# Order of loads and copies, and four banks of the first down product, in a two-layer decoder step

## The chip, the cores and the metric

The kernel is one program on one core of a Trainium2 chip. The metric is the time of one execution on the device, in microseconds. PE is TensorE, DVE is VectorE, ACT is ScalarE, POOL is GpSimd, and SP is SyncE, which here only issues the transfers.

## What is computed

One inference step of a decoder with two layers, for a prompt of 1024 tokens and 8 samples of 8 new tokens each that share the weights (width 1024, MLP width 4096). All data is float32.

```python
for layer in range(2):
    if layer == 0:   # one input projection; an mLSTM (4 heads) beside three dilated windowed attentions (8 heads each)
        mix_p = ab_output(h_a, oa, outs, lses, w_out_ab[j])          # prompt
        mix_s = ab_output(h_a, oa, outs, lses, w_out_ab[j])          # samples, with their caches
    else:            # windowed attention, 16 query heads on 2 key heads, with sinks
        mix_p = o.reshape(xp.shape[0], s_len, OUT_C) @ w_out_c[j]
        mix_s = o.reshape(xs.shape[0], t_len, OUT_C) @ w_out_c[j]
    xp = layer_norm(ALPHA * xp + mix_p, ln1_g[layer], ln1_b[layer])
    xp = layer_norm(ALPHA * xp + sq_relu_mlp(xp, w_up[layer], w_down[layer]), ln2_g[layer], ln2_b[layer])
    ...              # the same for xs
# sq_relu_mlp(x, w_up, w_down) = square(relu(x @ w_up)) @ w_down
```

The states and the keys and values to keep are outputs too.

## The kernel before, in words

The work is cut into stages, one after the other, each a block of five instruction streams (one for each engine) that meet at its end: the mLSTM; the three dilated attentions (tiles named `g_`); the samples' attention with the first output projection and norm (`sp_`); the first MLP (`f_`); the windowed attention (`c_`); its samples with the second output projection and norm (`wp_`); the second MLP (`f_` again). Tokens lie in nine tiles: eight prompt tiles of 128 rows and one sample tile of 64 rows, number NT = 8. Within a stage the order on each engine is the order of the code; semaphores hold an engine until another has come far enough. Eight PSUM banks are dealt out in fixed pools; PE can fill a bank only when DVE or ACT has emptied its last content.

Exact products come from splitting each factor: ACT rounds it (`hi`), DVE subtracts to get the rest (`lo`), and PE makes three passes. So every operand passes ACT and then DVE before PE can use it.

**Windowed attention** (lines 557 to 787). For tile n, PE computes scores, projects tile n + 1, transposes the input of tile n + 2, transposes the 32 probability blocks of tile n in 8 groups of 4 through the four banks of pool a (4 groups for tile 0), then the queries and keys of n + 1, then the weighted sum. ACT copies the even groups out, DVE the odd ones (lines 782 to 785). DVE's `x_rest(n + 2)` (line 780), the `lo` half of the input of tile n + 2, stands ahead of these copies. It isn't there for n = 7 and 8, which have no tile n + 2.

**First samples and projection** (lines 1954 to 2161). SP's loop over n issues, in this order: the stores of the sample result n - 1 to DRAM (`store_sample`, 8 small transfers), the loads for the merge, the store of the normed tile n - 2, the load of the residual input of tile n, then keys, mix and values. For n = 8 (`BD`) the samples' mix tile, which holds what was just stored, is loaded at line 2041, after all that, and behind the wait for the residual sum of tile 7 at line 2027. PE needs it for `mix_transposes(8)`, right after `project(7)`.

**Second samples and projection** (lines 1548 to 1848). SP loads the samples' projection, then mix tile 0, weight block 0, the samples' keys and values (1 MB), weight block 1, mix tile 1, weight block 2 (each block 1 MB, mix tiles 0.5 MB); block 3 follows when the first block is split (line 1568). ACT's order is fixed: mix tile 0, weight blocks 0 and 1, the copies of the transposed keys `kT` (lines 1716 to 1718), blocks 2 and 3. PE's scores need `kT`, and their first bank is one that these copies free.

**MLP** (lines 2373 to 2721). The hidden width goes in 16 groups of 256. PE makes `hidden(n)`, six units of 24 matmuls (two row blocks f by token ranges 0 to 383, 384 to 767, 768 to 1087), and `down(n)`, 18 banks (nine tiles by two halves of 512 columns), 6 matmuls in each, 4 for the sample tile; DVE adds each bank to the accumulator. The order is `hidden(0)`, `hidden(1)`, `down(0)`, `hidden(2)`, `down(1)` and so on, all after `hidden(0)` in a loop (line 2524). `hidden(1)` needs the up weights of group 1, which ACT can round only when `hidden(0)` has let go of the buffer. The tiles of `down` come in `ORDER` (line 2365): sample tile first, then 0 to 7. The last down product has its weights in the up buffers, so it waits until the last hidden product is through and they are split (`last_lo`); down product 14 covers four banks of that wait (lines 2530 to 2532). Then DVE adds and norms tile after tile in `ORDER`, with one fold more for the sample tile, and the stage ends with it.

Of the kernel before, what the change touches and what calls it, by code (L numbers as in the profile page):

```python
# [17 lines left out]
NT = SEQ // P  # L18
BD, TD = 8, 8
# [4 lines left out]
HB, DH = 8, 64  # L24
# [193 lines left out]
def attention(nc, env, name, groups, cfg):  # L218
# [13 lines left out]
    N = TILES * len(groups)  # L232
# [23 lines left out]
    def prob_banks(n):  # L256
        return H * spans(n) // 4
# [34 lines left out]
    with ExitStack() as ctx:  # L292
# [76 lines left out]
        with nc.Block() as block:  # L369
# [271 lines left out]
            def _(dve):  # L641
# [116 lines left out]
                for n in range(-1, N):  # L758
                    if attends(n):
                        maxima(n, 0)  # L760
                    if attends(n - 1):
                        o_out(n - 1)
                    if n >= 0 and n % TILES == NT and n + 1 < N:
                        rest_of_weights((n + 1) // TILES, 2)
                    if n + 1 < N:
                        z_out(n + 1, 0)
                        if n < 0:
                            if swa:
                                x_rest(1)
                            rest_of_weights(0, 2)  # L770
                        if attends(n) and HALVES == 2:
                            maxima(n, 1)
                        if (n + 1) % TILES == NT and n + 2 < N:
                            rest_of_weights((n + 2) // TILES, 0)
                        for c in range(1, NCH):
                            z_out(n + 1, c)
                            if c == (2 if swa else 1):
                                rope(n + 1)
                    if n + 2 < N and not (swa and n < 0):
                        x_rest(n + 2)  # L780
                    if attends(n):
                        for b in range(1, prob_banks(n), 2):
                            dve.wait_ge(*banks.full(n, "p", b))
                            dve.tensor_copy(pT[:, 4 * b:4 * b + 4, :].rearrange("p k t -> p (k t)"), bank(n, "p", b)[:, :])\
                                .then_inc(banks.free(n, "p", b)[0], 1)
                    if (n + 1) % TILES == NT and n + 2 < N:
                        rest_of_weights((n + 2) // TILES, 1)
# [668 lines left out]
def window_sample_and_projection(nc, env, cfg):  # L1456
# [7 lines left out]
    NTT = NT + 1  # L1464
# [24 lines left out]
    with ExitStack() as ctx:  # L1489
# [57 lines left out]
        with nc.Block() as block:  # L1547
            @block.sync
            def _(sp):
# [3 lines left out]
                def load_mix(n):  # L1553
                    sp.dma_start(mixt[n % 2][0:rows_of(n), :], cfg["mix"][n * P:n * P + rows_of(n), :]).then_inc(m_loaded[n % 2], 16)
# [2 lines left out]
                    sp.dma_start(staged(u), w_unit(cfg["wo"].rearrange("(k p) n -> p k n", p=P), u)).then_inc(w_loaded[u], 16)  # L1557

                sp.dma_start(new[:, :], cfg["zs"]).then_inc(new_loaded, 16)
                load_mix(0)  # L1560
                load_w(0)
                sp.dma_start(kv[:, :, :], cfg["cache"].rearrange("b s x h d -> s b (x h d)")).then_inc(kv_loaded, 16)
                load_w(1)
                load_mix(1)
                load_w(2)
                for h in range(HC):
                    sp.dma_start(sinkc[h * TD:(h + 1) * TD, :], cfg["sinks"][:, h:h + 1].to_broadcast([TD, 1])).then_inc(sink_loaded, 16)
                sp.wait_ge(w_lo, 1)
# [286 lines left out]
def sample_and_projection(nc, env, cfg):  # L1855
# [9 lines left out]
    NTT = NT + 1  # L1865
# [28 lines left out]
    with ExitStack() as ctx:  # L1894
# [58 lines left out]
        with nc.Block() as block:  # L1953
            @block.sync
            def _(sp):
# [62 lines left out]
                for n in range(NTT + 2):  # L2018
                    if 1 <= n <= BD:
                        store_sample(n - 1)  # L2020
                    if n + 1 < NT:
                        sp.wait_ge(products, n + 1)
                        load_groups(n + 1)
                    if n >= 2:
                        store(n - 2)
                    if 1 <= n < NTT:
                        sp.wait_ge(*banks.free(n - 1, "y", 1))
                        load_x(n)
                    if n + 2 < BD:
                        sp.wait_ge(*banks.full(n + 1, "k", NB - 1))  # L2030
                        load_keys(n + 2)
                    if n + 1 < NT:
                        sp.wait_ge(*banks.full(n, "m", 1))
                        load_mix(n + 1)
                    if n + 1 < BD:
                        sp.wait_ge(*banks.full(n, "o"))
                        load_values(n + 1)
                    if n == BD:
                        for par in range(2):
                            sp.wait_ge(ob_stored[par], 16 * HB * (BD // 2))  # L2040
                        load_mix(NT)
                        sp.wait_ge(*banks.full(BD - 1, "o"))
                        cfg["prefetch"](sp)
                        for m in range(4):
                            sp.wait_ge(stored[m % 2], 16 * (m // 2 + 1))
                            cfg["load_ahead"](sp, m)
# [315 lines left out]

NTOK = SEQ + NS
NPAD = (NT + 1) * P
ORDER = (NT,) + tuple(range(NT))
TOK_CHUNKS = [(0, 384), (384, 384), (768, 320)]
FG = 256
NFG = FF // FG
# [4 lines left out]
def mlp(nc, env, name, cfg):  # L2373
# [9 lines left out]
    with ExitStack() as ctx:  # L2383
# [45 lines left out]
        with nc.Block() as block:  # L2429
# [34 lines left out]
            def _(pe):  # L2464
# [40 lines left out]

                dn_flat = [w[:, :, :].rearrange("p f n -> p (f n)") for w in dn]

                def down(n, par):
                    pe.wait_ge(dn_lo.sem, dn_lo.done(n))
                    pe.wait_ge(h_lo.sem, h_lo.done(n, UP - 1))  # L2510
                    for b in range(DN):
                        pe.wait_ge(d_free.sem, d_free.done(n, b, back=4))
                        down_part(n, par, b, dn_flat, True, True).then_inc(d_full.sem, 1)

# [3 lines left out]
                for b in range(UP):  # L2518
# [2 lines left out]
                    hidden_unit(0, b)  # L2521
                    for n in ((4,), (5,), (6,), (7, 8), (), ())[b]:
                        x_transposes(n)
                with pe.Fori(0, NFG // 2 - 1) as i:
                    for par in range(2):
                        hidden(2 * i + par + 1)
                        down(2 * i + par, par)
# [14 lines left out]
            def _(act):  # L2542
# [46 lines left out]
                for b in range(UP + 1):  # L2589
                    if b < UP:  # L2590
                        relu(0, 0, b)
                    if b >= 1:
                        round_hidden(0, 0, b - 1)
                    for n in ((4,), (5,), (6,), (7, 8), (), (), ())[b]:
                        x_out(n)
                next_up(0)
                split_weights(0, dn_raw, dn[0], dn_loaded, None, dn_hi)
                with act.Fori(0, NFG // 2 - 1) as i:
                    for par in range(2):
                        step_(2 * i + par + 1, par ^ 1)  # L2600
# [24 lines left out]
            def _(dve):  # L2625
# [39 lines left out]
                            dve.tensor_tensor(a, a, d, ALU.add).then_inc(d_free.sem, 1)  # L2665

                def step_(n, par, first=False, more=True):
                    for b in range(UP):
                        hidden_rest(n + 1, par ^ 1, b)
                    dve.wait_ge(d_free.sem, d_free.done(n, 0, back=1))  # L2670
                    for i in range(NTT):
                        add(n, par, i, first)
                        if i == 2 and more:
                            rest(n + 2, up_raw, up, up_hi, up_lo)
                    rest(n + 1, dn_raw, dn, dn_hi, dn_lo)
# [16 lines left out]
                for b in range(UP):  # L2692
                    hidden_rest(0, 0, b)
                    for n in ((5,), (6,), (7, 8), (), (), ())[b]:
                        x_rest(n)
                rest(1, up_raw, up, up_hi, up_lo)
                rest(0, dn_raw, dn, dn_hi, dn_lo)
                dve.wait_ge(cleared, 1)
                step_(0, 0, first=True)
                with dve.Fori(0, NFG // 2 - 2) as i:  # L2700
# [239 lines left out]
```

## Time and profile before

| | |
|---|---|
| runs, median (lowest to highest) | 3292.88 us (3292.0 to 3296.89) |
| the profiled execution | 3288.4 us, its span 3286.6 us |
| PE matmul busy | 3071.8 us (93% of the span) |
| DVE busy | 1561.1 us (47%) |
| ACT busy | 902.1 us (27%) |
| mean granted TensorE clock | 0.959 |
| instructions | 46489 |

PE works nearly all the time, so what counts is the rest: stretches in which PE stands idle, and stretches at half clock. A matmul's busy time is longer than the distance to the next one, since they overlap; distances come from counts in a stretch. In a timeline row the bracket is the idle time before the instruction and what ended it.

### The profile page before, as it was taken

The numbers are of one execution on the slowest core, as the hardware profiler recorded it, in microseconds if no ns is written. First come the engines' busy times: TensorE is split into PE (matmuls) and PEld (weight loads), VectorE is DVE, ScalarE is ACT, GpSimd is POOL, SyncE is SP. The second block draws the span as 40 slices with busy tenths as digits, with TensorE's granted clock in tenths as the row PEclk, the third lists the DMA queues.
The fourth block names the chain that finished last, engine by engine and source line by source line (L and its number), as shares of the span: only waits on it lengthen the run. The fifth ranks groups of instructions, "written<-read, shape, count | busy, mean of one in ns | idle before, by whom it ended". The sixth has DMA issues, their size and how long they took to land. (4 is left out here: it accounts for less than half of the span.)

```text
span 3286.6 us, 46489 instructions
## 1 busy us (share of the span) xinstructions
PE 3071.8 (93%) x18199; PEld 2619.0 (80%) x18199; DVE 1561.1 (47%) x3277; ACT 902.1 (27%) x1905; POOL 195.0 (6%) x241
## 2 busy tenths in 40 slices
PE   8999699999996996999999999699797999999997
PEld 4666588788885875998999898588686899889986
DVE  1333543544435774344444446645554443444447
ACT  1222233333233433111121113444433111112113
POOL 0000000000000110100110010000000011001100
PEclk9999699999998997999999999899898999999999
DMA  6000231353788863110111011310421011101111
GB/s 212 20 19 16 52 130 45 113 202 132 262 262 282 284 220 109 52 51 29 48 51 51 26 64 43 119 38 28 152 87 39 26 51 51 51 26 51 51 38 68
DMA packets 134418, 300.09 MB, mean 91 GB/s; under 512 B 15048, under 2 KB 64392, under 8 KB 133192
## 3 DMA queue, kind: packets, MB, share of 16 engines
q1 hardware_dynamic: 134280, 298.19, 26.9%
q8 instruction: 93, 1.52, 0.2%
q14 instruction: 45, 0.37, 0.0%
HBM read 260.65 MB, written 93.34 MB: 108 GB/s over the span
## 5 line engine op out<-in xcount | busy, mean ns | idle before, releaser
L2482 PE MATMUL f_ps_u<-f_xT_hi,f_up_hi 128*128 128x384 f32 (+1 forms) x1536 | 507.9, 331 | 28.4 <-DVE f_up_lo L2637 12.1
L2482 PE MATMUL f_ps_u<-f_xT_hi,f_up_lo 128*128 128x384 f32 (+1 forms) x1536 | 506.3, 330 | 0.0
L2482 PE MATMUL f_ps_u<-f_xT_lo,f_up_hi 128*128 128x384 f32 (+1 forms) x1536 | 506.1, 329 | 0.0
L2652 DVE TENSOR_TENSOR f_hT_lo<-f_h,f_hT_hi 128x384 fp32r<-128x384 f32 (+1 forms) x192 | 146.1, 761 | 562.2 <-ACT f_hT_hi L2566 558.7
L2502 PE MATMUL f_ps_d<-f_dn_hi,f_hT_hi 128*128 128x512 f32 x1080 | 411.9, 390 | 1.3 <-DVE acc L2665 0.6
L2502 PE MATMUL f_ps_d<-f_dn_lo,f_hT_hi 128*128 128x512 f32 (+1 forms) x1080 | 411.7, 390 | 0.0
L2502 PE MATMUL f_ps_d<-f_dn_hi,f_hT_lo 128*128 128x512 f32 x960 | 373.9, 389 | 0.0
L2482 PEld LDWEIGHTS f_ps_u<-f_xT_hi,f_up_hi 128*128 128x128 f32 x1536 | 293.3, 191 | 31.2 <-issue 20.4
L2482 PEld LDWEIGHTS f_ps_u<-f_xT_lo,f_up_hi 128*128 128x128 f32 x1536 | 293.1, 191 | 1.1
L2482 PEld LDWEIGHTS f_ps_u<-f_xT_hi,f_up_lo 128*128 128x128 f32 x1536 | 292.8, 191 | 0.0
L2561 ACT ACTIVATE f_h<-f_ps_u 128x384 f32<-128x384 f32 (+1 forms) x192 | 91.0, 474 | 605.7 <-PE f_ps_u L2482 605.7
L524 PE MATMUL g_ps_b<-g_w_hi,g_xT_hi 128*128 128x512 f32 x648 | 255.3, 395 | 2.0 <-DVE g_xT_lo L655 2.0
L983 PE MATMUL m_ps_z<-w_m,m_xT 128*128 128x412 f32 (+3 forms) x800 | 248.7, 493 | 8.6 <-ACT m_xT L1106 5.9
L524 PE MATMUL g_ps_b<-g_w_lo,g_xT_hi 128*128 128x512 f32 (+1 forms) x648 | 251.8, 391 | 0.0
L2502 PEld LDWEIGHTS f_ps_d<-f_dn_hi,f_hT_hi 128*128 128x128 f32 x1080 | 202.8, 188 | 48.9 <-DVE acc L2665 1.9
L2502 PEld LDWEIGHTS f_ps_d<-f_dn_lo,f_hT_hi 128*128 128x128 f32 (+1 forms) x1080 | 196.3, 182 | 45.1
L2622 POOL TENSOR_TENSOR f_h<-f_h 128x384 f32<-128x384 f32 (+1 forms) x192 | 152.5, 794 | 1332.6 <-ACT f_h L2561 1332.6
L983 PEld LDWEIGHTS m_ps_z<-w_m,m_xT 128*128 128x128 f32 (+1 forms) x800 | 136.6, 187 | 114.3 <-issue 108.8
L524 PE MATMUL g_ps_b<-g_w_hi,g_xT_lo 128*128 128x512 f32 x576 | 225.4, 391 | 0.0
L2665 DVE TENSOR_TENSOR acc<-acc,f_ps_d 128x512 f32<-128x512 f32 x252 | 168.8, 686 | 104.1 <-PE f_ps_d L2502 104.1
L2502 PEld LDWEIGHTS f_ps_d<-f_dn_hi,f_hT_lo 128*128 128x128 f32 x960 | 180.2, 188 | 37.6
L2665 DVE TENSOR_TENSOR w_group<-w_group,f_ps_d 128x512 f32<-128x512 f32 x224 | 151.9, 686 | 102.6 <-PE f_ps_d L2502 102.6
(458 smaller groups left out, 4510.3 us busy)
## 6 DMA issues: line engine op xcount, KB each, us to landing
w_group<-in_w_in_ab SPq DMA_DIRECT2D x9, 2048.0 KB, 15.6
sample_keys<-in_w_up SPq DMA_DIRECT2D x16, 1024.0 KB, 7.3
sample_keys<-in_w_down SPq DMA_DIRECT2D x16, 1024.0 KB, 5.0
wo<-in_w_up SPq DMA_DIRECT2D x16, 1024.0 KB, 7.4
wo<-in_w_down SPq DMA_DIRECT2D x16, 1024.0 KB, 5.0
out<-in_cache_dil_kv SPq DMA_DIRECT2D x8, 2016.0 KB
g_xn<-in_x_prompt SPq DMA_DIRECT2D x16, 512.0 KB, 4.3
sample_keys<-in_cache_dil_kv SPq DMA_DIRECT2D x8, 1024.0 KB, 7.7
```

The lines of the kernel that those rows point to most:

```text
L524: last = pe.matmul(bank(n, "z", c)[0:w, 0:CHUNKS[c][0]], xp, wp, start=(k == 0 and q == 0), stop=(k == KT - 1 and q == len(passes) - 1))
L983: last = pe.matmul(out, xT[par][:, k, 0:out.shape[0]], W[:, k, a:b], start=(k == 0), stop=(k == KT - 1))
L2482: last = pe.matmul(ps_u[b % 3][:, 0:w], wp[:, k, f * P:(f + 1) * P], xp[:, k, t0:t0 + w], start=(k == 0 and q == 0), stop=(k == KT - 1 and ...
L2502: last = pe.matmul(bank[0:rows, :], hp, wp, start=(starts and f == 0 and q == 0), stop=(stops and f == FT - 1 and q == len(passes) - 1))
L2561: nc.scalar.activation(h[(par * UP + b) % 3][:, 0:w], ps_u[b % 3][:, 0:w], ACT.Relu).then_inc(relu_done.sem, 1)
L2622: pool.tensor_tensor(hs, hs, hs, ALU.mult).then_inc(squared.sem, 1)
L2652: last = dve.tensor_tensor(hT[par][1][:, f, t0:end], hs[:, 0:end - t0], as32(hT[par][0][:, f, t0:end]), ALU.subtract)
L2665: dve.tensor_tensor(a, a, d, ALU.add).then_inc(d_free.sem, 1)
```

## The change

Five edits: `x_rest(n + 2)` of the windowed attention goes between DVE's second and third copy; SP's start in the second projection stage gets another order; the load of the samples' mix tile in the first goes up; `ORDER` puts the sample tile third; and the first four banks of `down(0)` go between `hidden(0)` and `hidden(1)`, with the split of their weights earlier on ACT and DVE and the first pair of groups taken out of PE's loop.

```diff
 # windowed attention, DVE
-                    if n + 2 < N and not (swa and n < 0):
+                    if n + 2 < N and not (swa and (n < 0 or attends(n))):
                         x_rest(n + 2)
                     if attends(n):
                         for b in range(1, prob_banks(n), 2):
+                            if swa and b == min(5, prob_banks(n) - 1) and n + 2 < N:
+                                x_rest(n + 2)
 ...
 # second samples and projection, SP
+                sp.dma_start(kv[:, :, :], cfg["cache"].rearrange("b s x h d -> s b (x h d)")).then_inc(kv_loaded, 16)
                 load_mix(0)
-                load_w(0)
-                sp.dma_start(kv[:, :, :], cfg["cache"].rearrange("b s x h d -> s b (x h d)")).then_inc(kv_loaded, 16)
-                load_w(1)
                 load_mix(1)
-                load_w(2)
+                for u in range(3):
+                    load_w(u)
 ...
 # first samples and projection, SP, right after store_sample(n - 1)
+                    if n == BD:
+                        sp.wait_ge(*banks.full(NT - 1, "m", 1))
+                        for par in range(2):
+                            sp.wait_ge(ob_stored[par], 16 * HB * (BD // 2))
+                        load_mix(NT)
 ...
-                        for par in range(2):
-                            sp.wait_ge(ob_stored[par], 16 * HB * (BD // 2))
-                        load_mix(NT)
 ...
 # MLP
-ORDER = (NT,) + tuple(range(NT))
+ORDER = (0, 1, NT) + tuple(range(2, NT))
+EARLY = 4
 ...
-                def down(n, par):
+                def down(n, par, units=range(DN)):
                     pe.wait_ge(dn_lo.sem, dn_lo.done(n))
-                    pe.wait_ge(h_lo.sem, h_lo.done(n, UP - 1))
-                    for b in range(DN):
+                    pe.wait_ge(h_lo.sem, h_lo.done(n, UP - 1 if units[-1] >= EARLY else FT - 1))
+                    for b in units:
 ...
-                with pe.Fori(0, NFG // 2 - 1) as i:
+                down(0, 0, range(EARLY))
+                hidden(1)
+                down(0, 0, range(EARLY, DN))
+                hidden(2)
+                down(1, 1)
+                with pe.Fori(1, NFG // 2 - 1) as i:
 ...
 # ACT, in the loop over the units b of hidden(0)
+                    if b == 3:
+                        split_weights(0, dn_raw, dn[0], dn_loaded, None, dn_hi)
                 next_up(0)
-                split_weights(0, dn_raw, dn[0], dn_loaded, None, dn_hi)
 ...
 # DVE, step_ and the same loop
+                    if first:
+                        for i in range(EARLY // 2):
+                            add(n, par, i, first)
 ...
-                    for i in range(NTT):
+                    for i in range(EARLY // 2 if first else 0, NTT):
 ...
+                    if b == 3:
+                        rest(0, dn_raw, dn, dn_hi, dn_lo)
                 rest(1, up_raw, up, up_hi, up_lo)
-                rest(0, dn_raw, dn, dn_hi, dn_lo)
```

## Rows read from the trace of the kernel before

**Rows 1.** Stretch, length, busy PE, PEld, DVE, ACT, POOL (count), clock, DMA share, GB/s.
```profile
1331.00:2008.00 677.00, 677.00 (x3556) 615.20 (x3555) 301.86 (x400) 130.86 (x205) 69.34 (x88) 1.00 0.13 42
```

**Rows 2.** Waits of PE over the whole run: total, times, longest.
```profile
PE f_ps_u L2482 <- DVE f_up_lo L2637: 12.1, 2, 6.0
...
PE c_ps_a L472 <- DVE c_pT L784: 10.8, 7, 2.0
...
PE sp_ps_t L2057 <- DMA sp_mixt<-mix: 5.8, 1, 5.8
...
PE wp_ps_k L1608 <- DMA wp_kv<-in_cache_swa_kv: 4.1, 1, 4.1
```

**Rows 3.** Timeline of the windowed attention: start, duration, engine, operation, idle before.
```profile
2177.72 1.28 DVE L655 TENSOR_TENSOR c_xT_lo<-c_ps_c,c_xT_hi 128x512 fp32r<-128x512 f32 x2
...
2178.92 1.28 DVE L784 COPY c_pT<-c_ps_a 128x512 f32<-128x512 f32 x2
...
2179.75 1.50 PE L472 MATMUL c_ps_a<-consts,c_prob 128*128 128x128 f32 x12 [1.53 <-DVE c_pT L784]
```

**Rows 4.** Timeline of the first sample and projection stage, its last two tiles.
```profile
1221.26 2.67 SPq L1998 DMA_DIRECT2D mix<-sp_ob  x8
...
1231.79 0.69 DVE L2304 SCALAR_TENSOR_TENSOR sp_io<-sp_io,sp_ps_y 128x512 f32<-128x512 f32 x1 [4.56 <-PE sp_ps_y L2104]
...
1233.13 0.53 SPq L1987 DMA_DIRECT2D sp_mixt<-mix  x1
...
1237.48 1.11 PE L2057 MATMUL sp_ps_t<-consts,sp_mixt 64*128 64x64 f32 x8 [5.84 <-DMA sp_mixt<-mix]
...
1239.56 0.76 PE L2104 MATMUL sp_ps_y<-sp_wo_hi,sp_mT_hi 128*128 128x512 f32 x1 [0.97 <-DVE sp_mT_hi L2295]
```

**Rows 5.** Stretches as in rows 1: projection, product starts, steady down products, first products.
```profile
1239.50:1244.80 5.30, 5.24 (x12) 3.48 (x13) 4.47 (x9) 3.78 (x5) 0.00 (x0) 0.50 1.03 403
1314.60:1320.00 5.40, 5.35 (x17) 5.35 (x18) 2.11 (x1) 0.00 (x0) 0.00 (x0) 0.50 0.26 99
2529.20:2535.20 6.00, 5.92 (x18) 5.92 (x19) 2.14 (x1) 0.00 (x0) 0.00 (x0) 0.50 0.44 128
1342.00:1362.00 20.00, 20.00 (x90) 16.41 (x89) 13.42 (x20) 2.27 (x2) 0.38 (x1) 1.00 0.00 1
1269.80:1308.70 38.90, 34.30 (x184) 33.38 (x184) 10.13 (x16) 8.54 (x20) 4.03 (x5) 0.84 0.09 28
2487.00:2523.30 36.30, 31.73 (x184) 30.82 (x184) 10.13 (x16) 8.51 (x20) 4.03 (x5) 0.91 0.10 29
```

**Rows 6.** Timeline where the first MLP goes from group 0 to group 1.
```profile
1305.14 0.44 ACT L2561 ACTIVATE f_h<-f_ps_u 128x320 f32<-128x320 f32 x1 [6.52 <-PE f_ps_u L2482]
...
1306.01 0.78 DVE L2652 TENSOR_TENSOR f_hT_lo<-f_h,f_hT_hi 128x384 fp32r<-128x384 f32 x1 [6.13 <-ACT f_hT_hi L2566]
...
1312.22 2.29 DVE L2637 TENSOR_TENSOR f_up_lo<-sample_keys,f_up_hi 128x2048 fp32r<-128x2048 f32 x1 [1.24 <-ACT f_up_hi L2547]
1314.43 2.29 DVE L2637 TENSOR_TENSOR f_dn_lo<-sample_keys,f_dn_hi 128x2048 fp32r<-128x2048 f32 x1
...
1314.65 0.68 PE L2482 MATMUL f_ps_u<-f_xT_hi,f_up_hi 128*128 128x384 f32 x1 [6.03 <-DVE f_up_lo L2637]
```

**Rows 7.** Timeline of DVE in the tail of the second MLP.
```profile
3227.08 0.69 DVE L2665 TENSOR_TENSOR acc<-acc,f_ps_d 128x512 f32<-128x512 f32 x1 [0.17 <-PE f_ps_d L2502]
```

**Rows 8.** Timeline of DVE in a down product of the first MLP.
```profile
1490.54 0.69 DVE L2665 TENSOR_TENSOR w_group<-w_group,f_ps_d 128x512 f32<-128x512 f32 x1 [0.67 <-PE f_ps_d L2502]
...
1493.34 1.96 DVE L2665 TENSOR_TENSOR w_group<-w_group,f_ps_d 128x512 f32<-128x512 f32 x3
```

**Rows 9.** Timeline at the start of the second sample and projection stage.
```profile
2350.15 1.90 ACT L1709 CAST wp_wo_hi<-wo 128x2048 fp32r<-128x2048 f32 x1 [3.32 <-DMA wo<-in_w_out_c]
...
2351.96 1.07 ACT L1718 COPY wp_kT<-wp_ps_k 128x512 f32<-128x512 f32 x2
...
2353.26 3.42 PE L1653 MATMUL wp_ps_k<-wp_knT,wp_qT 128*128 128x8 f32 x16
```

## The prediction

> **What bounds the kernel now.** I looked first at the busy time of each engine, then at what it is in stretches. PE is busy 677.00 of 677.00 us from the second pair of groups to the last of the first MLP, at full clock [rows 1]; DVE is at 45% there. Loops of this kind can't gain, so the change can only win where PE stands idle or runs at half clock. PE's waits, longest first, give the places that the five edits touch [rows 2]: 12.1 us in two waits before group 1 of the MLPs (6.0 each), 10.8 us in seven waits for DVE's probability copies, 5.8 us for the samples' mix tile, 4.1 us for the samples' keys. The chain of waits is mostly "issue" and says no more. For each place I read the timelines of all engines around it.
>
> **Part 1, windowed attention.** PE's sixth group of transposes needs the bank that DVE's first copy empties. DVE starts that copy only after `x_rest`: 2177.72 plus 1.2 us, so 2178.92 [rows 3]. PE waits 1.53 us for it. Of the seven waits the last (2.0 us, the longest in rows 2) is that of tile 7, which has no `x_rest`; it stays. The other six sum to 10.8 - 2.0 = 8.8 us. With `x_rest` after two copies, the first copy starts 1.2 us sooner, and of 1.53 us some 0.33 stay: 8.8 - 6 x 0.33 = 6.8 us. What is late next: `x_rest` itself ends at 2180.35, and its bank is wanted by the weighted sum, which now starts at about 2181.6, after the query and key transposes; copies 5 and 7 end at 2181.0 and 2181.7, and the weighted sum wants them only in its second half. DVE's total is unchanged. Tile 0 has four groups and no such wait: 0. Bounds: 0, if the wait only moves to the weighted sum, and 8.8. I take 6.8.
>
> **Part 2, the samples' mix tile.** SP's last eight stores of sample results end their issue at 1221.26 + 2.67 = 1223.9; the mix tile is issued at 1233.13, and PE can transpose it at 1237.48, 4.35 us later [rows 4]. Between the two SP sat behind the residual sum of tile 7 (first instruction at 1231.79). Now it waits for the stores to land and issues at once. No row has the landing of these small stores; I bound it by 0 and by the 4.35 us of that load. So the tile is there between 1228.3 and 1232.6, and PE is through with `project(7)` at about 1231.65 (it idled 5.84 us up to 1237.48). At the worst 1.0 us is left; I take none. From the first transpose to the first matmul of the last projection went 2.08 us (1237.48 to 1239.56), so that starts at 1233.7: 5.9 us gained. It also ran at half clock, 12 matmuls in 5.30 us [rows 5], where 12 take 2.7 at full clock (below): with no gap but the 1 us for the split I expect the clock to stay, 2.6 us more. Sum 8.5 us, bounds 4.9 and 8.5. SP's wait delays the store of tile 6 and the load of the samples' x by at most 1.7 us; nobody wants that store's buffer for 20 us, and the load is behind the residual sum anyway. What ends the stage is DVE's norm of the last tile, whose chain starts from this projection, and it moves with it. The weights and tiles fetched for the MLP still start at about 1233.
>
> [...]
>
> **Part 3, four banks before group 1.** A down matmul of 512 columns comes every 0.227 us or so (90 in 20.00 us, counting those cut by the edges) [rows 5]. Four banks of two prompt tiles are 24: 5.4 us.
> - When can they start? `hidden(0)` ends 6.03 us before 1314.65, at 1308.6 [rows 6]. The rounding of the down weights (1.9 us, as the cast in rows 9) now lies in ACT's 6.52 us of idleness before 1305.14. DVE's part (2.29 us) follows the unit at 1306.01, so 1306.8 to 1309.1, just ahead of DVE's next unit at 1309.5: hidden. The banks run from 1309.1 to 1314.5.
> - When can `hidden(1)` start? Its weights are ready at 1312.22 + 2.29 = 1314.5, as before. So it starts at the same 1314.65, but with 24 matmuls done: 5.4 us, in each layer.
> - The clock: after the idle 6 us the next 5.4 us of layer 0 and 6.0 us of layer 1 ran at 0.50 [rows 5]. With 0.5 us of idleness in its place, half of these comes back: 2.7 and 3.0 us.
> - SP: `load_dn(1)` is issued some 7 us sooner, on empty queues; no one waits.
> - The loop loses its first pass, which now stands as straight code, some 500 matmuls. Rows 1 cover seven loop passes with no idle PE, so a back edge costs nothing there; for straight code the nearest rows are the first products [rows 5], whose idle 4.6 us of 38.90 have other causes; 0 taken, 4.6 us as the bound.
> - Tail: the order puts tile 0 first. After the gate `last_lo` PE must make 12 matmuls before DVE has two full banks, where the sample tile needs 8. DVE waited for that second bank (0.17 us before 3227.08 [rows 7]), and from there it works without a pause to the end. So its chain starts 4 x 0.227 = 0.9 us later, in both layers; the gate doesn't move, since it hangs on `hidden(15)`. The sample fold (about 2 us) is only moved.
> Sum: 5.4 + 2.7 - 0.9 = 7.2 and 5.4 + 3.0 - 0.9 = 7.5, together 14.7 us. Bounds for both: 4 (clock not regained, split late) and 18.
>
> The Trainium skill (Runtime: NRT & Kernel Launch, Instruction fetch mechanics) says that a taken branch whose target is outside the two fetched pages stalls, and that straight code is prefetched. By it the peeled pass would save a stall in each layer; rows 1 show none, and I book 0.
>
> **Part 4, order within steady products.** The sample tile's short banks move from first to third. DVE's 2.3 us split of the next up weights still comes after six banks, 7.3 us into the product either way. Before it bank 5 is full at about 1490.5; after it the add of bank 6 ends at 1494.0 [rows 8]; PE wants that bank at 1490.5 + 4 x 1.36 = 1495.9. The spare 1.9 us stays. 0.
>
> **Part 5, second projection stage.** Before weight block 1 now come 0.5 MB more (mix tile 1). At 390 GB/s, what a 1 MB transfer in 2.6 us makes (blocks at about 2344.9 and 2350.15 with the keys between), that is 1.3 us: ACT rounds it at 2351.5 instead of 2350.15 [rows 9], and `kT`, queued behind it, is copied at 2353.3 instead of 2351.96. The first score bank is free with the first of the two copies, 2353.9; PE started there at 2353.26. The keys' own wait of 4.1 us goes, but PE then waits here. So +0.7 us. Block 3 is issued 2.6 us later and rounded by 2364; PE wants it at about 2369. Bounds: 4.1 us gained, 3 lost (with longer half clock). I take 0.7 lost.
>
> **The sum.** 6.8 + 8.5 + 14.7 - 0.7 = 29.3 us off the profiled execution, 3288.4 (span 3286.6): 3259.1. The median of the runs is 4.5 us above that execution, so 3292.9 - 29.3 = 3263.6 us. The stages follow each other, so the parts add.
>
> **Rivals.**
> - A: the attention's waits move. DVE is the same 5 instructions in another order; if copies 5 and 7 hold the weighted sum, Part 1 gives 0: 3270.4. For it: both wait on DVE; against: PE has 12 transposes of other tiles between.
> - B: clock. The first MLP spent 38.90 us on its first product and the second 36.30 on the same matmuls, clock 0.84 and 0.91 [rows 5]: the clock falls after some gaps of 2 us and not after others. If the early banks run at half clock they take 24 x 0.44 = 10.5 us and `hidden(1)` starts 5 us late in both layers: 3273.7.
> - C: the down weights' split is late, and the early banks start only when those of `hidden(1)` are ready: they no longer fill the gap, and of Part 3 only -0.9 and part of the clock stays, about +12: 3275.6. Against: 6.52 us idle ACT, and 2.29 us fit before 1309.5 with 0.4 to spare.
> - D, slower: the accumulation becomes the bound. If the new order makes DVE's add of bank 6 later by more than the spare 1.9 us, PE stalls in each of 15 products of two layers, 30 times. Each us beyond costs 30; from 1.0 us beyond the gain is gone, at 1.3 it is 3263.6 + 39 = 3302.6. Against: the banks ahead of the split sum to the same time.
>
> **How the numbers follow.** Forecast 0.73, A 0.10, B 0.08, C 0.05, D 0.02, the change does less than it says in two places at once (about 3284) 0.02. The forecast's own spread is the clock's 2.6 us per layer, Part 5's bounds and the runs' own; 3256 to 3273. The range takes A and B and most of C: 3256 to 3279. A difference of 0.2% is 6.6 us, about what can be told from no change: faster needs under 3286.3. That holds in all cases but D and a part of the last, with some room for what I have not seen: faster 0.95, same 0.03, slower 0.02.
>
> **What would show it.** PE's waits for `c_pT` at 4 us in all instead of 10.8; none for `sp_mixt`, and the last `sp_` projection at clock 1.00; no 6 us wait for `f_up_lo`, 24 down matmuls before `hidden(1)`, and 1.00 behind them; DVE's tail 0.9 us longer from the gate; PE's first `wp_` score 0.7 us later from the stage's start. Wrong would be: waits of PE in the loops (D), or a `wp_` stage that is several us off.

## The result and the profile after

| | before | changed |
|---|---|---|
| median of the runs (lowest to highest) | 3294.89 us (3292.0 to 3304.87, 4 runs) | 3262.34 us (3259.86 to 3265.96, 4 runs) |
| span of the profiled execution | 3286.6 us | 3260.9 us |
| mean granted clock | 0.959 | 0.963 |
| PE matmul busy | 3071.8 us | 3064.5 us |

The ratio is 0.9898, 95% interval 0.9883 to 0.9914: 1.0% faster. Forecast were 3263.6 us and faster. A second measurement of the changed kernel, beside other runs, gave a median of 3258.65 us and a ratio of 0.9892 (0.9865 to 0.9918).

The waits of PE over the whole run, in the columns of [rows 2]:

```profile
PE wp_ps_k L1654 <- ACT wp_kT L1719: 4.8, 1, 4.8
...
PE c_ps_a L472 <- DVE c_pT L786: 4.2, 7, 2.0
```

The 12.1 us for `f_up_lo` ahead of group 1 and the 5.8 us for `sp_mixt` are gone from the list. The wait for `c_pT` fell from 10.8 to 4.2 us, of which 2.0 are tile 7's; in place of 4.1 us for the samples' keys stand 4.8 us for `kT`.

The windowed attention, the same places of a tile as [rows 3]:

```profile
2164.72 1.28 DVE L786 COPY c_pT<-c_ps_a 128x512 f32<-128x512 f32 x2
...
2165.55 1.50 PE L472 MATMUL c_ps_a<-consts,c_prob 128*128 128x128 f32 x12 [0.34 <-DVE c_pT L786]
...
2165.92 1.28 DVE L655 TENSOR_TENSOR c_xT_lo<-c_ps_c,c_xT_hi 128x512 fp32r<-128x512 f32 x2
...
2168.53 1.64 PE L552 MATMUL c_ps_c<-c_pT,c_v 128*64 128x128 f32 x26
```

DVE now copies first and runs `x_rest` (L655) behind two copies; PE's wait is 0.34 us instead of 1.53, and `x_rest` is through at 2167.2, before the weighted sum (L552) starts. For the first five tiles that have an `x_rest`, PE's wait is the same 1.53 us before and 0.34 now, and it comes every 29.07 us where it came every 30.27; at the sixth (tile 6) it was only 1.09 and is 0.43.

The first sample and projection stage, as [rows 4]:

```profile
1225.92 2.67 SPq L1999 DMA_DIRECT2D mix<-sp_ob  x8
...
1229.55 0.51 SPq L1988 DMA_DIRECT2D sp_mixt<-mix  x1
...
1236.21 0.71 PE L2060 MATMUL sp_ps_t<-consts,sp_mixt 64*128 64x64 f32 x8
...
1236.42 0.69 DVE L2307 SCALAR_TENSOR_TENSOR sp_io<-sp_io,sp_ps_y 128x512 f32<-128x512 f32 x1 [4.53 <-PE sp_ps_y L2107]
...
1237.97 0.47 PE L2107 MATMUL sp_ps_y<-sp_wo_hi,sp_mT_hi 128*128 128x512 f32 x1 [1.05 <-DVE sp_mT_hi L2298]
```

The last stores are issued by 1228.59 and the load at 1229.55: the wait for their landing took 0.96 us. PE goes from `project(7)` into the transposes without idling.

Where the first MLP goes from group 0 to group 1, as [rows 6]:

```profile
1302.44 2.28 DVE L2647 TENSOR_TENSOR f_dn_lo<-sample_keys,f_dn_hi 128x2048 fp32r<-128x2048 f32 x1
...
1304.77 0.50 PE L2506 MATMUL f_ps_d<-f_dn_hi,f_hT_hi 128*128 128x512 f32 x1 [0.42 <-DVE f_dn_lo L2647]
...
1307.95 2.29 DVE L2647 TENSOR_TENSOR f_up_lo<-sample_keys,f_up_hi 128x2048 fp32r<-128x2048 f32 x1 [1.25 <-ACT f_up_hi L2556]
...
1310.35 0.39 PE L2486 MATMUL f_ps_u<-f_xT_hi,f_up_hi 128*128 128x384 f32 x1
```

The split of the down weights ends at 1304.72, the last matmul of `hidden(0)` starts at 1304.04, and the first early bank at 1304.77, after a wait of 0.42 us for that split. `hidden(1)` starts at 1310.35, 6.31 us behind the start of that last matmul, where it was 6.34: as late as before, but with 24 down matmuls done. Its own weights are split at 1310.24 (1307.95 + 2.29), so the 24 fill the wait almost exactly.

Stretches as in [rows 1] and [rows 5]: the loop over the groups, the last projection, the early banks, the first microseconds of `hidden(1)` in both layers:

```profile
1315.00:1991.00 676.00, 676.00 (x3566) 616.53 (x3565) 299.43 (x392) 129.46 (x205) 70.61 (x89) 1.00 0.12 42
1237.90:1243.10 5.20, 5.13 (x22) 3.65 (x23) 4.36 (x9) 3.73 (x5) 0.00 (x0) 1.00 0.93 273
1304.70:1310.30 5.60, 5.53 (x24) 4.43 (x25) 3.76 (x7) 2.74 (x4) 0.72 (x1) 1.00 0.55 187
1310.30:1316.00 5.70, 5.70 (x34) 5.70 (x34) 2.34 (x4) 0.49 (x1) 0.67 (x1) 1.00 0.57 184
2510.90:2516.90 6.00, 6.00 (x35) 5.79 (x34) 2.70 (x5) 0.49 (x1) 0.60 (x1) 1.00 0.55 175
```

The loop stays full. The 24 early matmuls run at full clock. The projection and the two starts of `hidden(1)` stood at 0.50 before and stand at 1.00: 22 matmuls of the projection in 5.2 us, where 12 took 5.3.

DVE in the tail of the second MLP, as [rows 7], and the start of the second projection stage, as [rows 9]:

```profile
3200.06 0.69 DVE L2675 TENSOR_TENSOR acc<-acc,f_ps_d 128x512 f32<-128x512 f32 x1 [1.88 <-PE f_ps_d L2506]
3201.37 0.69 DVE L2675 TENSOR_TENSOR acc<-acc,f_ps_d 128x512 f32<-128x512 f32 x1 [0.62 <-PE f_ps_d L2506]
```

```profile
2332.91 1.90 ACT L1710 CAST wp_wo_hi<-wo 128x2048 fp32r<-128x2048 f32 x1 [0.81 <-DMA wo<-in_w_out_c]
...
2334.72 1.07 ACT L1719 COPY wp_kT<-wp_ps_k 128x512 f32<-128x512 f32 x2
...
2335.44 3.56 PE L1654 MATMUL wp_ps_k<-wp_knT,wp_qT 128*128 128x8 f32 x16 [4.79 <-ACT wp_kT L1719]
```

In the tail DVE idles 0.62 us ahead of the second bank, where it idled 0.17. In the projection stage the keys are transposed by 2329.8, but `kT` waits on ACT behind the rounding of two weight blocks until 2334.72.

**The whole, cut into stretches.** Distances between starts of named matmuls, in us, from the timelines. In the first three rows no instruction of PE is edited.

| stretch | before | changed | difference |
|---|---|---|---|
| start to first transpose of the dilated attention | 409.39 | 410.78 | +1.39 |
| to the first transpose of the `sp_` stage | 618.25 | 619.26 | +1.01 |
| to the last matmul of `project(7)` | 203.62 | 205.85 | +2.23 |
| to the last matmul of `project(8)` (Part 2) | 18.04 | 9.29 | -8.75 |
| first MLP, first to last up matmul (Parts 3, 4) | 733.89 | 725.28 | -8.61 |
| from there to the first matmul of the next stage | 65.35 | 66.27 | +0.92 |
| windowed attention (Part 1) | 262.81 | 256.16 | -6.65 |
| to the first matmul of the second projection (Part 5) | 28.04 | 28.82 | +0.78 |
| first to last matmul of that projection | 109.55 | 109.37 | -0.18 |
| second MLP, first to last up matmul | 731.54 | 722.84 | -8.70 |
| from there to the start of the last instruction | 67.98 | 68.91 | +0.93 |

The two hand-overs into the MLPs (20.6 and 17.6 us) differ by less than 0.1. The edited stretches sum to -30.3 us, forecast -29.3; the 4.6 us that the first three rows lost take the span's difference to 25.7.

The trace of the second measurement has the attention at 256.13 us, the second MLP at 722.84 and the tails at 66.26 and 68.93, as in the table. Its first MLP took 722.45, 2.8 less, all of it in the first product: `hidden(0)` took 35.48 us at a mean clock of 0.91, in the table's trace 38.31 at 0.84. Over the 14 traces of this document that first product took 35.5 to 39.6 us with and without the edits, so what the MLP edit brings is read behind it.

### The profile page after: what moved, and what is told of

Its sections match the earlier page's. It is cut to its first block and busy times, and to the rows that moved or that the text cites. A ratio compares the mean times of both kernels' runs of the same rounds, so it can differ in the third digit from the quotient of the medians.

```text
span 3260.9 us, 46391 instructions
## 1 busy us (share of the span) xinstructions
PE 3064.5 (94%) x18199; PEld 2611.2 (80%) x18199; DVE 1561.2 (48%) x3277; ACT 901.6 (28%) x1905; POOL 194.7 (6%) x241
```

## The experiments

Each run leaves a trace, and the stretch that an edit touches is compared in it. A median can't tell a few microseconds: the stretch from the first `sp_` transpose to `project(7)`, in which PE's code is the same in all 14 traces, was 202.9 to 211.4 us long.

### One part at a time

The change has four places (the two edits of the MLP count as one); each was put into the kernel before alone, with the diff shown above for it.

**The attention edit.**

> Kernel before with the attention edit alone. My theory: PE's sixth group of transposes waits 1.2 us less for DVE's first copy in each of six tiles, so a tile takes 29.07 us instead of 30.27, the waits for c_pT are 4.2 us instead of 10.8, and the span falls by 6.7 us (3286.6 to 3279.9); all stages behind it keep their lengths. Rival A (the waits only move to the weighted sum, which then waits for copies 5 and 7): a tile still takes 30.27 us, 0. A rival on the sum (the whole gain comes from the clock of later stages): then this one shows nothing.

Measured: 0.9972 (0.9957 to 0.9988). The attention took 257.69 us instead of 262.81, and the wait is down:

```profile
PE c_ps_a L472 <- DVE c_pT L786: 4.1, 7, 2.0
```

So it is 5.1 to 6.7 us (the kernels without the edit have 262.7 to 264.5 here, those with it 256.1 to 257.7), on its own. The span itself didn't fall (3288.9): `sp_` had 7.6 us more in this execution. Rival A, by which a tile would still take 30.27 us, is out.

**The samples' mix tile.**

> Kernel before with the earlier load of the samples' mix tile alone. My theory: no wait of PE for sp_mixt, and the last projection at full clock; from the last matmul of project(7) to the last of project(8) 9.2 us instead of 18.0, span 8.8 us less, the MLP behind it unchanged. Rival (the store of tile 6 and the loads that now queue behind SP's wait come late): the start of the MLP after the last projection moves by more than 0.5 us from 20.56, and the gain is under 7. The 2.2 us that the samples' attention took longer in the changed kernel, before this place, belong to the run and not to the edit: the stretch from the first sp_ transposes to the end of project(7) is 203.6 +- 1 us here, if they belong to the edit it is 205.8.

Measured: 0.9965 (0.9948 to 0.9982). `project(7)` to `project(8)` 9.30 us, as in every kernel with this edit, against 16.9 to 18.4 in those without; the way on to the MLP 20.55. The stretch ahead of `project(7)` was 205.6 here, which is the value that the expectation had set for a loss by the edit. More traces say otherwise: the eight traces with the edit have 204.3 to 210.6 (mean 206.8), the six without it 202.9 to 211.4 (mean 207.1), so the 2.2 us of the table are scatter.

**The MLP.**

> Kernel before with the MLP edits alone (order of tiles, four early banks, early split, first pass of the loop unrolled). My theory: 5.4 us of matmuls in a gap and 3.0 us of clock in each layer, less 0.9 us in each tail: span 15.5 us less, 3271.1, of which 7.7 and 7.8 in the two MLPs and nothing elsewhere. Rival B (the early banks at half clock): 5 us less gain in all per layer. Rival C (split late): gain near 2.

Measured: 0.9931 (0.9907 to 0.9955). First to last up matmul 725.07 and 722.91 us, tails 66.27 and 68.87: gains 7.9 and 7.7 us. The interval of the median reaches from 15 to 31 us off and holds them at its edge.

**The loads of the second projection stage.**

> Kernel before with the order of loads of the second projection stage alone. My theory: 0.5 to 0.8 us slower, all of it before the first projection (28.8 us after the attention's last matmul instead of 28.0), because the copies of kT stand behind two weight blocks on ACT; the wait of 4.1 us for the samples' keys becomes one of 4.8 us for kT. The rival (the edit is worth up to 4.1 us and the changed kernel's number for it is spoilt by something else): span 3 to 4 us less. In time a difference of 0.02% can't be told; the trace's stretch decides.

Measured: 0.9996 (0.9978 to 1.0014), which tells nothing. The stretch ahead of the first projection was 28.43 us here, and is 28.4 to 28.9 in the six traces (this one among them) with the edit and the old order on ACT, 27.5 to 28.4 in the six without: about 0.6 us slower on average. The wait is the one expected:

```profile
PE wp_ps_k L1652 <- ACT wp_kT L1717: 4.8, 1, 4.8
```

The spans of these four executions (3288.9, 3287.7, 3279.4 and 3291.3 us, in the kernel before 3286.6) didn't fall by what was expected of them, since stretches that the edit doesn't touch moved by up to 7.7 us. The gains of the parts rest on the stretches alone.

### What in the MLP edit brings the time

**The split left late.** On ACT and DVE the changed kernel's two lines go back behind the up weights:

```diff
-                    if b == 3:
-                        split_weights(0, dn_raw, dn[0], dn_loaded, None, dn_hi)
                 next_up(0)
+                split_weights(0, dn_raw, dn[0], dn_loaded, None, dn_hi)
 ...
-                    if b == 3:
-                        rest(0, dn_raw, dn, dn_hi, dn_lo)
                 rest(1, up_raw, up, up_hi, up_lo)
+                rest(0, dn_raw, dn, dn_hi, dn_lo)
```

> Changed kernel, but the down weights of group 0 are rounded and subtracted behind the up weights of group 1 on ACT and DVE, as in the kernel before. My theory (the gain is matmuls that fill the gap, and the clock that is kept by them): the early banks start only 2.1 us after the old start of group 1, so PE idles 8.4 us between its two products instead of 0.7, and the half clock behind it is back (3.0 us): 7.7 + 3.0 = 10.7 us per layer, span 21.4 us longer than the changed kernel's 3260.9. If only the idle time counts and the clock of those microseconds has another cause: 15.4. Rival C's mechanism priced by this: the changed kernel without its early split would gain about 12 us against the kernel before. A rival by which straight code in place of the loop's first pass brings the gain: less than 5 us slower than the changed kernel.

Measured: median 3281.49 us, 0.9969 (0.9958 to 0.9979) of the kernel before. Its waits, and the early banks' stretches:

```profile
PE f_ps_d L2506 <- DVE f_dn_lo L2646: 16.3, 2, 8.1
```

```profile
1308.00:1315.30 7.30, 7.30 (x24) 5.92 (x25) 2.07 (x3) 0.00 (x0) 0.00 (x0) 0.74 0.87 284
2519.40:2526.90 7.50, 7.50 (x24) 6.01 (x25) 2.07 (x3) 0.00 (x0) 0.00 (x0) 0.72 0.77 279
```

PE waits 8.1 us in each layer. `hidden(1)` starts 15.81 and 15.99 us behind the last matmul of `hidden(0)`, in the changed kernel 6.31 and 6.32: 9.5 and 9.7 us per layer, not 10.7. The idle time is the 7.7 expected. Of the clock 1.8 and 2.0 came, since only part of the banks ran at half clock (0.74 and 0.72 of the full clock over them) and `hidden(1)` at full. So the early split is what makes the early banks worth anything; with it late, the MLPs are no faster than before (732.3 and 732.5 us, and without their first products 1.0 us slower in both). The span is 15.5 us above the changed kernel's and not 19.2, mostly because the first `hidden(0)` took 2.5 us less in this execution (35.85 us at a mean clock of 0.91 instead of 38.31 at 0.84). The rival with straight code is out, since this kernel has that code too.

**Two banks instead of four** (`EARLY = 2`):

> Changed kernel with two early banks instead of four: 12 matmuls (2.7 us) in the gap, so about 3.1 us idle before group 1. The fill term alone: 2.7 us per layer, 5.4 in all slower than the changed kernel. The clock: rows of the kernel before show half clock after idle stretches of 2.5 us in some places (1286.0 to 1289.4) and none after one of 1.8; so I expect 1.7 us of half clock per layer more, 8.8 in all. If the clock were lost as after the 6 us gap: 11.4 in all; if kept: 5.4.

Measured: median 3270.58 us. First to last up matmul 728.02 and 725.59 us, so 2.74 and 2.75 more than in the changed kernel, 5.5 in all: the 12 matmuls (2.7 us) and nothing else.

```profile
PE f_ps_u L2486 <- DVE f_up_lo L2647: 5.1, 2, 2.5
```

```profile
1312.10:1318.10 6.00, 5.96 (x34) 5.96 (x35) 1.18 (x2) 0.49 (x1) 0.83 (x1) 1.00 0.56 175
2516.40:2522.40 6.00, 5.94 (x34) 5.94 (x35) 1.21 (x3) 0.49 (x1) 0.83 (x1) 1.00 0.57 178
```

PE idles 2.5 us here ahead of `hidden(1)`, and the clock stays at 1.00 in both layers. My 8.8 us was too much: the clock's part of the gain isn't in proportion to the filling; half of it was enough for all of the clock.

**Straight code, and the order of the tiles,** each alone in the kernel before:

```diff
+                for par in range(2):
+                    hidden(par + 1)
+                    down(par, par)
-                with pe.Fori(0, NFG // 2 - 1) as i:
+                with pe.Fori(1, NFG // 2 - 1) as i:
```

> Kernel before with only the first pass of PE's loop over the groups written out ahead of it, the order of the matmuls unchanged. My theory: 0 (within 0.3 us in each MLP, by the stretch from the first up matmul to the last: 733.9 and 731.5 us). The Trainium skill (Runtime: NRT & Kernel Launch, Instruction fetch mechanics) has taken branches stall where their target isn't fetched, so one back edge less per MLP would make each stretch shorter; the traces show no idle PE there.

Measured: 3290.7 us in a single run; 732.80 and 731.48 us. The first is 1.1 less than before, which the expectation excluded, but that lies in `hidden(0)` (37.39 us at a mean clock of 0.86 instead of 38.46 at 0.84), ahead of the edit. From the last matmul of `hidden(1)` to the last up matmul it is 662.95 us in both kernels and both layers: 0.00.

```diff
-ORDER = (NT,) + tuple(range(NT))
+ORDER = (0, 1, NT) + tuple(range(2, NT))
```

> Kernel before with only the order of the tiles changed (0, 1, sample tile, 2 to 7). My theory: nothing in the steady products (stretch from first to last up matmul 733.9 and 731.5 us within 0.3), 0.9 us more from the last up matmul to the end of each MLP (65.35 to 66.3 to the first matmul behind the first MLP; 67.98 to 68.9 to the span's end), because DVE's first two banks behind the last weights hold 12 instead of 8 matmuls: 1.8 us slower. Rival D (the add of bank 6 later than its spare 1.9 us): waits of PE on DVE in each of 15 products, tens of us slower.

Measured: 3294.99 us in a single run. Tails 66.27 and 68.88: +0.92 and +0.90, as expected. First to last up matmul it is 733.16 and 732.86 us, 0.7 less and 1.3 more than before and so not within the 0.3 expected; the larger differences lie in the clock of the first two hidden products (the second layer's `hidden(0)` took 38.72 us instead of 35.89, its `hidden(1)` 25.33 instead of 26.36). Between the last matmul of `hidden(1)` and the last up matmul it is 662.48 us in both layers instead of 662.95: 0.47 less, which wasn't forecast. PE has no new wait for DVE there.

The traces show where the 0.47 us arise. A steady hidden product takes 23.70 us in both kernels, a steady down product 23.66 us before and 23.62 now. Where the sample tile's eight matmuls open the product they start 233 ns apart on average, in third place 229 ns (28 products in each trace), which is all of the 0.034 us; 14 products make the 0.47. Why the first place costs these matmuls more is open.

### The attention once more

`x_rest` behind all of DVE's copies instead of between the second and third:

```diff
                         for b in range(1, prob_banks(n), 2):
-                            if swa and b == min(5, prob_banks(n) - 1) and n + 2 < N:
-                                x_rest(n + 2)
                             dve.wait_ge(*banks.full(n, "p", b))
 ...
+                        if swa and n + 2 < N:
+                            x_rest(n + 2)
```

> Changed kernel, but x_rest of the windowed attention goes behind all of DVE's probability copies instead of between the second and third. It tests what I named as late next, the weighted sum, which overwrites the bank that x_rest reads. In the changed kernel x_rest ends at 2167.2 and the weighted sum starts at 2168.53, 1.3 us later. Behind the copies x_rest would end at about 2168.9: if the weighted sum waits for both halves of it, a tile takes up to 0.4 us more than 29.07 (2.5 us in six tiles); if only for the first half, 0. Rival A's reading (copies 5 and 7 are what the weighted sum waits for): with both copies 1.2 us sooner a tile gets shorter than 29.07.

Measured: 3265.04 us in a single run; the attention 256.58 us, PE's wait every 29.07 us. DVE and PE at the end of a tile's copies:

```profile
2169.29 0.69 DVE L784 COPY c_pT<-c_ps_a 128x512 f32<-128x512 f32 x1 [0.18 <-PE c_ps_a L472]
...
2169.90 1.28 DVE L655 TENSOR_TENSOR c_xT_lo<-c_ps_c,c_xT_hi 128x512 fp32r<-128x512 f32 x2
...
2170.73 1.97 PE L552 MATMUL c_ps_c<-c_pT,c_v 128*64 128x128 f32 x32
```

The weighted sum starts 0.4 us before `x_rest` is through and without idle time ahead of it, so it doesn't wait for both halves. Copies 5 and 7 done sooner don't shorten the tile either. With DVE's first two copies ahead, the two orders tried take the same time.

### A better version

Two edits on top of the changed kernel: on ACT the copies of `kT` ahead of weight blocks 0 and 1, and the old order of the tiles for the last two down products.

```diff
                 mix_out(0)
-                weights(0)
-                weights(1)
                 for i in range(2):
                     act.wait_ge(*banks.full("k", i))
                     nc.scalar.copy(kT[:, seqs(i), :], blocks(bank("k", i))).then_inc(banks.free("k", i)[0], 1)
+                weights(0)
+                weights(1)
 ...
+LAST = (NT,) + tuple(range(NT))
 ...
 # and so wherever the last two down products and the tail took ORDER
-                for i, m in enumerate(ORDER):
+                for i, m in enumerate(LAST):
```

> Changed kernel with two more edits, in separate stages. (1) ACT copies the transposed keys kT before it rounds weight blocks 0 and 1: the transposes of the keys end at 2329.8 and block 0 is rounded from 2330.2, so the scores can start at 2331.1 instead of 2335.4 and the first projection follows when they are through and block 0 and 1 are split: 3.4 us sooner (25.2 us after the attention's last matmul instead of 28.6). If the first projection is set by the blocks' arrival instead, the gain is 0. (2) The last two down products of each MLP take the tiles in the old order, sample tile first: 0.92 us back in each tail, 1.8 in all. Together 5.2 us less than the changed kernel.

Measured: 3258.62 us, 0.9887 (0.9858 to 0.9916); the changed kernel measured beside it 3258.65. The tails are 65.35 and 67.95, as before the change: 1.9 us back. The first matmul of the projection starts 20.83 us behind the attention instead of 28.8, 8.0 us sooner, and from there to its last it takes 117.88 us instead of 109.4: all given back. Its waits and its clock:

```profile
PE wp_ps_k L1609 <- ACT wp_prob L1725: 4.0, 1, 4.0
...
PE wp_ps_y L1635 <- DVE wp_wo_lo L1768: 2.1, 1, 2.1
```

```profile
2347.70:2354.50 6.80, 4.68 (x15) 4.08 (x16) 4.29 (x11) 6.33 (x20) 0.00 (x0) 0.52 0.25 71
```

PE waits 2.1 us for weight block 3 inside the projection, then 4.0 for ACT's exponentials, and 6.8 us at half clock follow. DVE's timeline shows why the exponentials are late; the maxima that they need stand behind the split of block 3 (and behind the rest of mix tile 1):

```profile
2339.59 2.29 DVE L1768 TENSOR_TENSOR wp_wo_lo<-wo,wp_wo_hi 128x2048 fp32r<-128x2048 f32 x1 [3.09 <-ACT wp_wo_hi L1710]
...
2344.53 1.29 DVE L1795 TENSOR_REDUCE wp_mx<-wp_prob 128x8 f32<-128x1088 f32 x1
```

Hence one more edit:

```diff
                 rest_of_weights(2)
+                maxima()
                 rest_of_weights(3)
                 mix_rest(1)
-                maxima()
```

> The kernel of the run ktfirst_tail with one more edit: DVE takes the maxima of the samples' scores ahead of the split of weight block 3 instead of behind it. That run won 8.0 us up to the first projection and lost 8.5 behind it: PE idled 2.4 us for block 3 inside the first projection, then 4.0 us until ACT's exponentials, whose maxima stood on DVE behind block 3, which lands only at 2337.6; and half clock followed. My theory: the scores are there at 2331.5, the maxima run from 2336.5 to 2340.0, the exponentials end at 2344, before PE asks for them at 2347; the wait of 4.0 us and the half clock behind it (6.8 us, 3.4 lost) go, block 3 is split 0.4 us later. So 7 us less than ktfirst_tail in this stage (129.3 instead of 138.7 + 8.0 - 8.0, that is: first to last projection about 112 us instead of 117.9, with 20.9 + 0.0 to 0.4 ahead of it), span 5.5 to 7 us under that run's where the rest is equal. Rival: the clock is lost all the same by the 2.4 us for block 3, then 4 us less. A further rival: what sets the samples' probabilities is the exponentials behind block 3 on ACT, then 0 to 1.

Measured: 3260.32 us (3248.17 to 3262.59), 0.9885 (0.9864 to 0.9906). First to last matmul of the projection 111.54 us with 20.89 ahead: 132.4 us, where the changed kernel has 138.2 and ktfirst_tail 138.7; 6.3 us of the 7 expected. The wait for the exponentials is gone, 2.3 us for block 3 are left, and the clock stays:

```profile
PE wp_ps_y L1635 <- DVE wp_wo_lo L1768: 2.3, 1, 2.3
```

```profile
2339.00:2360.00 21.00, 18.70 (x92) 15.42 (x91) 18.47 (x29) 13.13 (x30) 0.00 (x0) 1.00 0.70 251
```

By its stretches this version is 5.8 + 1.9 = 7.6 us better than the changed kernel. Its median doesn't show that: the intervals of the ratio are 0.4% wide or more, and its profiled execution (span 3259.0 us) had 3.4 us more than the changed kernel's in the samples' attention, 1.3 in the first MLP's first product and 1.5 in the windowed attention, none of which differ between the two kernels. That it beats the changed kernel in time is therefore not shown.

## Why the prediction was right

The time (3262.34 for 3263.6) is nearer than the working deserves, and that is luck: the forecast takes 29.3 us off, the median fell by 32.6 (the median before was 3294.9 in the comparison, not the 3292.9 of the forecast), and the span of the profiled executions by 25.7, since the changed kernel's had 4.6 us more in stretches without an edit. The stretches are the fair test.

- Part 1: 6.8 forecast, 6.65 in the trace. The waits of the six tiles, 8.8 us in all, are 2.2. They aren't six equal ones as the sum took them: five fell by 1.19 us each (1.53 to 0.34), the sixth by 0.66 (1.09 to 0.43). That `x_rest` and the copies are then in time was read right; xlast shows even more room.
- Part 2: 8.5 forecast, 8.75. Of these 5.9 us are the wait, as forecast, 2.5 the projection's clock for 2.6, and 0.3 the transposes and their split, which no term had. The stores' landing, which no row gave, took at most 0.96 us of the 0 to 4.35 allowed, so the tile was in time.
- Part 3: 7.2 and 7.5 forecast, and 7.7 and 7.8 measured. The measured ones hold the order's 0.47 us, and in the first layer 0.15 us of `hidden(0)`; without them it is 7.1 and 7.3. The matmuls in the gap are 24 at 0.227 us, 5.4. The clock gave back 2.55 and 2.78 us (`hidden(1)` takes 23.6 us instead of 26.14 and 26.36), where 2.7 and 3.0 stood; among the twelve cases without the MLP edit two had less half clock to give back (25.0 us in swa_only, 25.33 in order_only, second layer). The tails cost 0.92 and 0.93 for 0.9. The early split was ready 0.42 us after PE wanted it, as the 0.5 us of idleness in the forecast had it; latesplit shows that 9.6 us a layer hang on its being there. Rival B didn't come, since the early banks ran at 1.00 (24 matmuls in 5.6 us), and C didn't, since they started 0.42 us late and not behind the weights of `hidden(1)`.
- Part 4: 0 forecast; the order gives 0.47 us in each MLP, in the sample tile's own matmuls (see order_only). The term was put at nothing because only DVE's spare time was looked at.
- Peeled pass: 0 booked, 0.00 found. By the rule of the Trainium skill (Runtime: NRT & Kernel Launch, Instruction fetch mechanics) that a taken branch stalls when its target isn't in the fetched pages, one back edge less could have saved a stall. The trace shows none: 662.95 us with it and without. Whether the loop's target lay outside the fetched pages, no run shows.
- Part 5: 0.7 lost forecast, 0.78 in the trace up to the first projection, 0.64 up to the first score, and 0.6 over twelve traces. The reason named, `kT` behind weight block 1, is the wait that the trace shows. What I had left out is how much of the stage hung on that order of ACT: 8 us to the first projection, though without the maxima's move none of it is kept.
- Rival D: no waits of PE in the loops, so the spare time of bank 6 held.

Of the expectations two were too high, both in the clock: I priced half clock as if the next product had to pay for it (latesplit) or in proportion to idle time (early2). The rows that early2's expectation cites have shorter gaps than it says: PE idles 2.2 us ahead of 1285.1, and the 2.5 us are the idle time of the weight loads. One was too low: for ktfirst_tail I took 3.4 us to the first projection where 8.0 came, since the scores then also ran at full clock (16 matmuls in 1.85 us instead of 3.56, and the next 16 in 2.03 instead of 3.76), and I looked at the first projection alone, not at what is late behind it.

## What to carry over

Fill a gap with work whose operands can be ready, and move the preparation of these operands with it: the early banks without their early split are worth nothing. A wait removed at a stage's start is only won when the whole chain behind it is early too; look at what each engine's fixed order (here DVE's maxima behind a weight block) holds back. And with terms of a few microseconds compare stretches of the trace, not medians or spans: one unedited stretch scattered by 8 us from execution to execution.

## What the runs showed of the hardware

- The clock behind waits of PE: after the one of 5.9 to 6.0 us `hidden(1)` began at 0.50 in both layers of each of the six traces that have it (the kernel before, swa_only, sp_only, wp_only, peel, order_only), and stayed there for 3.0 to 6.0 us; after one of 2.5 us (early2) it stayed at 1.00 in both layers, and after 2.3 us in a projection too (maxfirst); after 2.1 and then 4.0 us (ktfirst_tail) it fell for 6.8 us. The wait alone doesn't decide: in the kernel before, PE's idle times of 2.2 us ahead of 1285.1 and ahead of 2501.2 came with 3.4 us at 0.50 (from 1286.0 and from 2501.1), and one of 2.25 us ahead of 2515.95 with none.
- Eight small stores to DRAM (2 KB each, issued by SyncE) had landed 0.96 us after the issue of the last had ended (1228.59 to 1229.55), or sooner.
- 24 down matmuls at 1.00 took 5.6 us, the same 24 with the clock at 0.72 to 0.74 took 7.4 and 7.5 us (latesplit).
- The sample tile's down matmuls start 233 ns apart as the first of a product and 229 ns as the third tile's, at full clock (the kernel before and order_only, 28 products each).
